# Stick-breaking sums in the rounded four-byte format, from a high and a low part of the softplus

## The reference, cut to what matters

```
z = jnp.einsum('bhqd,bhkd->bhqk', qb, kb) * scale
strict = k_pos < q_pos
log_keep = jnp.where(strict, jax.nn.log_sigmoid(-z), 0.0)
prefix = jnp.cumsum(log_keep, axis=-1)
after = prefix[..., -1:] - prefix
w = jnp.where(strict, jnp.exp(jax.nn.log_sigmoid(z) + after), 0.0)
outs.append(jnp.einsum('bhqk,bhkd->bhqd', w, vb))
```

## Time and profile before

| what | value |
|---|---|
| median of 3 runs | 1195.76 us (1193.81 to 1197.41) |
| the profiled run's own time | 1202.31 us |
| its span, first to last instruction | 1200.7 us |
| mean granted TensorE clock | 0.999 of full |
| TensorE matmuls, busy | 1185.0 us, 99% of the span |
| VectorE, ScalarE, GpSimd busy | 863.5, 636.0 and 95.4 us |

### The profile page before, as it was taken

The page is one execution under the profiler, slowest core; times in us unless marked ns, Lnnn a source line. Parts: engine busy times, 40 slices in busy tenths (PEclk is TensorE's granted clock), DMA queues, the critical chain, the costliest instruction groups (busy, mean ns, idle before and its releaser), DMA issues.

```text
span 1200.7 us, 23381 instructions
## 1 busy us (share of the span) xinstructions
PE 1185.0 (99%) x9643; PEld 1148.8 (96%) x9643; DVE 863.5 (72%) x1143; ACT 636.0 (53%) x853; POOL 95.4 (8%) x147
## 2 busy tenths in 40 slices
PE   8999999999999999999999999999999999999998
PEld 8999999999998999999999999999988779999998
DVE  5776887778776897777899888886476557755443
ACT  7557566634447567634468464333455665543432
POOL 0000010110124011110200001110000000000000
PEclk9999999999999999999999999999999999999999
DMA  9442587887772588787844648876745406565361
GB/s 335 159 175 72 178 290 269 297 291 253 263 263 72 176 270 291 277 289 275 294 171 141 203 149 281 286 254 204 235 142 193 157 1 187 166 210 178 124 193 66
DMA packets 150009, 249.98 MB, mean 208 GB/s; under 512 B 5505, under 2 KB 80618, under 8 KB 149930
## 3 DMA queue, kind: packets, MB, share of 16 engines
q1 hardware_dynamic: 135810, 198.21, 49.1%
q0 software_dynamic: 13952, 50.60, 11.7%
q10 hardware_dynamic: 168, 0.04, 0.0%
HBM read 247.79 MB, written 1.05 MB: 207 GB/s over the span
## 4 chain that ended last, share of the span: by engine, by line
PE 88%; DVE 8%; ACT 2%; issue 1%; ACTq 0%; POOL 0%; DVEq 0%
PE ps L2137 26%; PE ps L2139 26%; PE ps L2138 26%; DVE w_lo L1252 4%; PE ps L2405 2%; PE ps L2275 1%; PE ps L2693 1%; DVE scratch L1729 1%; PE ps L2387 1%; PE ps L2191 1%; ACT h_both L804 1%; PE ps L2667 1%; PE ps L2374 1%; PE ps L2707 1%; PE ps L2218 0%
## 5 line engine op out<-in xcount | busy, mean ns | idle before, releaser
L1252 DVE TENSOR_TENSOR w_lo<-raw,w_hi 128x2048 fp32r<-128x2048 f32 (+4 forms) x196 | 412.6, 2144 | 103.0 <-ACT w_hi L737 102.8
L737 ACT ACTIVATE w_hi<-raw 128x2048 fp32r<-128x2048 f32 (+4 forms) x196 | 342.0, 1790 | 169.0 <-PE ps L2139 168.9
L2137 PE MATMUL ps<-h_both,w_hi 128*128 128x256 f32 (+1 forms) x1296 | 363.8, 281 | 2.9 <-issue 1.1
L2139 PE MATMUL ps<-h_both,w_lo 128*128 128x256 f32 (+1 forms) x1296 | 361.3, 279 | 0.0
L2138 PE MATMUL ps<-h_both,w_hi 128*128 128x256 f32 (+1 forms) x1296 | 361.3, 279 | 0.0
L2137 PEld LDWEIGHTS ps<-h_both,w_hi 128*128 128x128 f32 (+1 forms) x1296 | 242.7, 187 | 4.3 <-issue 3.8
L2138 PEld LDWEIGHTS ps<-h_both,w_hi 128*128 128x128 f32 (+1 forms) x1296 | 244.2, 188 | 0.1
L2139 PEld LDWEIGHTS ps<-h_both,w_lo 128*128 128x128 f32 (+1 forms) x1296 | 244.1, 188 | 0.0
L2137 PE MATMUL ps<-a_both,w_hi 128*128 128x256 f32 x864 | 242.1, 280 | 0.0
L2139 PE MATMUL ps<-a_both,w_lo 128*128 128x256 f32 x864 | 241.4, 279 | 0.0
L2138 PE MATMUL ps<-a_both,w_hi 128*128 128x256 f32 x864 | 241.3, 279 | 0.0
(11 more groups left out here) (420 smaller groups left out, 1823.6 us busy)
## 6 DMA issues: line engine op xcount, KB each, us to landing
ada_raw<-in_l_ada_w POOLq DMA_DIRECT2D x96, 512.0 KB, 6.7
raw<-in_mlp_w_up SPq DMA_DIRECT2D x32, 1024.0 KB, 6.9
raw<-in_mlp_w_down SPq DMA_DIRECT2D x32, 1024.0 KB, 6.8
raw<-in_l_ffn_w_gate SPq DMA_DIRECT2D x22, 1024.0 KB, 5.4
raw<-in_l_ffn_w_up SPq DMA_DIRECT2D x22, 1024.0 KB, 8.0
raw<-in_l_ffn_w_down SPq DMA_DIRECT2D x16, 768.0 KB, 6.0
raw<-in_l_w_qkv SPq DMA_DIRECT2D x12, 1024.0 KB, 7.0
raw<-in_l_w_in SPq DMA_DIRECT2D x10, 1024.0 KB, 6.5
```

The costliest lines, as they stand in the source:

```text
L737: nc.scalar.activation(w_hi[:, s.slot, cut], raw[:, s.slot, cut], ACT.Copy).then_inc(split_hi, 1)
L1252: nc.vector.tensor_tensor(w_lo[:, s.slot, cut], raw[:, s.slot, cut], w_hi[:, s.slot, cut].bitcast(F32), ALU.subtract).then_inc(split_lo, 1)
L2137: nc.tensor.matmul(to, sh, mh, start=first, stop=False, skip_group_check=True)
L2139: return nc.tensor.matmul(to, sl, mh, start=False, stop=last, skip_group_check=True)
```

## The change

The softplus is split in a high part, rounded to `F32R`, and a low part, the rest. The sums become products of these two parts with constants in `F32R`: four products for each head, where there were two in the plain format.

- GpSimd copies each head's softplus into `sp_hi` (rounded) once `sp_ready` tells that it is there, and increments `sp_high`. From the third head on it first waits for the sums of the head two before.
- VectorE has a new step `softplus_low`: `sp_lo` = `sb_sp` - `sp_hi`, increments `sp_low`. Its order in iteration p is now `softplus(p + 1)`, `capped(p + 2)`, `softplus_low(p + 1)`, then `mix_low` as before.
- TensorE waits for `sp_low` in place of `sp_ready`, and uses `denied` in place of `suffix`.
- `sb_l` is gone: its steps work in `sb_w`, which has 8 places for heads in place of 4. `sb_sp`, `sp_hi` and `sp_lo` have 2 each. The waits on places are changed to match.
- `minus_ones` is made by a `tensor_scalar` in `F32R`, from `ones`, in place of a memset.

```
-            nc.gpsimd.memset(minus_ones[:, :], -1.0).then_inc(pool_step, 1)
+            nc.gpsimd.tensor_scalar(minus_ones[:, :], ones[:, :], -1.0, None, ALU.mult).then_inc(pool_step, 1)
...
+            for h in range(SB_HEADS):
+                pool.wait_ge(sp_ready, h + 1)
+                if h >= 2:
+                    pool.wait_ge(sums_ready, h - 1)
+                nc.gpsimd.tensor_copy(sp_hi[:, h % 2, :], sb_sp[:, h % 2, :]).then_inc(sp_high, 1)
...
-                    if h >= 4:
-                        dve.wait_ge(sp_ready, h - 3)
-                    nc.vector.tensor_scalar(sb_l[:, h % 4, :], ps[:, STICK_BANKS[h % 6], 0:384], FULL, None, ALU.min).then_inc(z_capped, 1)
+                    if h >= 8:
+                        dve.wait_ge(heads_done, len(HEADS) + h - 7)
+                    nc.vector.tensor_scalar(sb_w[:, h % 8, :], ps[:, STICK_BANKS[h % 6], 0:384], FULL, None, ALU.min).then_inc(z_capped, 1)
...
-                    if h >= 4:
-                        dve.wait_ge(sums_ready, h - 3)
-
-                    nc.vector.tensor_tensor(sb_sp[:, h % 4, :], ps[:, STICK_BANKS[h % 6], 0:384], sb_l[:, h % 4, :], ALU.max)                        .then_inc(sp_ready, 1)
+                    if h >= 2:
+                        dve.wait_ge(sp_low, h - 1)
+
+                    nc.vector.tensor_tensor(sb_sp[:, h % 2, :], ps[:, STICK_BANKS[h % 6], 0:384], sb_w[:, h % 8, :], ALU.max)                        .then_inc(sp_ready, 1)
+
+            def softplus_low(pair):
+
+                for h in (2 * pair, 2 * pair + 1):
+                    dve.wait_ge(sp_high, h + 1)
+                    nc.vector.tensor_tensor(sp_lo[:, h % 2, :], sb_sp[:, h % 2, :], sp_hi[:, h % 2, :].bitcast(F32), ALU.subtract)\
+                        .then_inc(sp_low, 1)
 
             capped(0)
             capped(1)
             softplus(0)
+            softplus_low(0)
             for p in range(SB_PAIRS):
                 if p + 1 < SB_PAIRS:
                     softplus(p + 1)
                 if p + 2 < SB_PAIRS:
                     capped(p + 2)
+                if p + 1 < SB_PAIRS:
+                    softplus_low(p + 1)
...
-                pe.wait_ge(sp_ready, h + 1)
-                z, sp_of = ps[:, STICK_BANKS[h % 6], :], sb_sp[:, h % 4, :]
-                nc.tensor.matmul(z[:, 0:384], suffix[:, :], sp_of, start=False, stop=False, skip_group_check=True)
-                nc.tensor.matmul(z[:, P:T], minus_ones[:, :], sp_of[:, T:T + P], start=False, stop=True,
-                                 skip_group_check=True).then_inc(sums_ready, 1)
+                pe.wait_ge(sp_low, h + 1)
+                z = ps[:, STICK_BANKS[h % 6], :]
+                for sp_of in (sp_hi[:, h % 2, :], sp_lo[:, h % 2, :]):
+                    nc.tensor.matmul(z[:, 0:384], denied[:, :], sp_of, start=False, stop=False, skip_group_check=True)
+                    ins = nc.tensor.matmul(z[:, P:T], minus_ones[:, :], sp_of[:, T:T + P], start=False, stop=False, skip_group_check=True)
+                ins.then_inc(sums_ready, 1)
```

More of the change, by code:

```diff
@@ L309, in build @@
         sb_kT = at("sb_kT", 8192, [P, KD, T])
[L310 to L316, removed]
+        sb_w = at("sb_w", 10240, [P, 8, 384])
+        sb_sp = at("sb_sp", 13312, [P, 2, 384])
+        sp_hi = at("sp_hi", 14080, [P, 2, 384], F32R)
+        sp_lo = at("sp_lo", 14848, [P, 2, 384], F32R)
+        suffix = at("suffix", 15616, [P, P])
+        minus_ones = at("minus_ones", 15744, [P, P], F32R)
+        denied = at("denied", 15872, [P, P], F32R)
+        far = at("far", 16000, [P, P], F32R)
         sb_sq = at("sb_sq", 12800, [P, NT, BANK])
@@ L370, in build @@
             sem("qk_sq"), sem("qk_var"), sem("qk_y"), sem("qk_scaled"), sem("qk_turned"), sem("qk_out"))
-        z_ready, z_capped, z_exped, z_soft, sp_ready, sums_ready, w_exped = (
-            sem("z_ready"), sem("z_capped"), sem("z_exped"), sem("z_soft"), sem("sp_ready"), sem("sums_ready"), sem("w_exped"))
+        z_ready, z_capped, z_exped, z_soft, sp_ready, sp_high, sp_low, sums_ready, w_exped = (
+            sem("z_ready"), sem("z_capped"), sem("z_exped"), sem("z_soft"), sem("sp_ready"), sem("sp_high"), sem("sp_low"),
+            sem("sums_ready"), sem("w_exped"))
         q_out, k_out, qk_banks = sem("q_out"), sem("k_out"), sem("qk_banks")
@@ L1198, in soft @@
                     act.wait_ge(z_capped, h + 1)
-                    nc.scalar.activation(sb_l[:, h % 4, :], sb_l[:, h % 4, :], ACT.Exp).then_inc(z_exped, 1)
+                    nc.scalar.activation(sb_w[:, h % 8, :], sb_w[:, h % 8, :], ACT.Exp).then_inc(z_exped, 1)
                 for h in (2 * pair, 2 * pair + 1):
                     act.wait_ge(z_exped, h + 1)
-                    nc.scalar.activation(sb_l[:, h % 4, :], sb_l[:, h % 4, :], ACT.Ln, bias=1.0).then_inc(z_soft, 1)
+                    nc.scalar.activation(sb_w[:, h % 8, :], sb_w[:, h % 8, :], ACT.Ln, bias=1.0).then_inc(z_soft, 1)
             def weights(pair):
@@ L1207, in weights @@
                     act.wait_ge(sums_ready, h + 1)
-                    if h >= 4:
-                        act.wait_ge(heads_done, len(HEADS) + h - 3)
-                    nc.scalar.activation(sb_w[:, h % 4, :], ps[:, STICK_BANKS[h % 6], 0:384], ACT.Exp).then_inc(w_exped, 1)
+                    nc.scalar.activation(sb_w[:, h % 8, :], ps[:, STICK_BANKS[h % 6], 0:384], ACT.Exp).then_inc(w_exped, 1)
             for j in range(6):
@@ L2707, in sb_values @@
                         ins = nc.tensor.matmul(ps[rows_of, 6 + g % 2, to], sb_rows[:, 2, kt, h * HD:(h + 1) * HD],
-                                               sb_w[:, h % 4, cut], start=pair % 2 == 0 and kt == 0, stop=pair % 2 == 1 and kt == 1,
+                                               sb_w[:, h % 8, cut], start=pair % 2 == 0 and kt == 0, stop=pair % 2 == 1 and kt == 1,
                                                skip_group_check=True)
```

## The result

The changed kernel took 1201.33 us in the median of 20 runs (1198.11 to 1206.97), the kernel before 1196.38 on the same chip: a ratio of 1.0041, 95% interval 1.0026 to 1.0056. It is slower by 0.4%, 4.95 us. The forecast was 1198.0 within 1193.5 to 1201.5, so the median is 3.3 us above it, 0.17 under the upper end of the range. Two further timings of the same pair on other chips gave ratios of 1.0002 (0.9983 to 1.0021) and 1.0035 (1.0012 to 1.0058).

What follows compares the result with a forecast made beforehand. TensorE was taken to bound the kernel, busy 99% of the span. First iteration +1.0, iterations 1 to 5 +1.0 and end +0.2 made +2.2: 1204.5 profiled, less 6.55 for the median, 1198.0 us, range 1193.5 to 1201.5.

Steps and rivals of the forecast that it cites:

- The loop: Attention iterations: sums, scores to `capped`, two `capped`, then subtraction and semaphore form one chain of 4.20 us, against 4.02.
- the two `capped`: VectorE, in the iteration's chain: two `capped` before the next instruction take 0.99 us.
- First iteration: Iteration 0 of the attention: 4.01 us against 3.02, adding 1.0 us.
- The products: TensorE sums: a head costs 0.57 us instead of 0.87, with 0.11 for each 128-column rounded product.
- Rival 2: TensorE sums: a rounded 128-column product costs 0.22 us, making the loop 4.64 and the time 1201.1; chance 0.17.
- the bound of 0.06: TensorE sums: lower bound in us for a rounded 128-column product, a third of the 384 columns' 0.17.
- The copies: GpSimd: 16 copies of 128 x 384 at 0.64 us each, hidden except at the end.
- rival 3: GpSimd copies are slow, 1.17 us each, adding 3.5 us in all, to 1199.3; chance 0.08.
- The end: Attention from 976.48 on: 6.3 us against 6.12, with the last subtraction waiting beside GpSimd's second copy.
- Rival 1: Attention: TensorE stays the limit and cheaper products save 4.8 us, giving 1191.0; chance 0.09.
- Rival 4, the clock: TensorE's clock falls to 1.2 GHz in new gaps, some 2.6 us in each of six iterations; chance 0.02.
- the forecast's own mark of 0.3%: Whole kernel: faster or slower means a difference of over 0.3%, 3.6 us; anything less counts as same.

Runs made afterwards that it cites:

- scores_first: Changed kernel with TensorE's order made scores, sums, values from iteration 1 and VectorE's made capped, softplus, low part; ratio to the kernel before 0.9967.
- copy_twice: Changed kernel with each GpSimd copy made twice, the second waiting on the first; attention 33.76 us against 30.30, no timed ratio given.
- before_scores_first: Kernel before (plain products) with the orders of scores_first, at one look; attention 28.37 and 28.36 us in this kernel's two runs.
- scores_first_pe: Changed kernel with only TensorE's order altered (scores, sums, values from iteration 1), VectorE's order kept; ratio to the kernel before 0.9995, attention 24.95 us.
- after_third: Changed kernel, unchanged, timed again on the same chip as filled_again; ratio to the kernel before 1.0035.
- filled: Changed kernel with TensorE's gaps filled by unused 128-column products, 12 in iteration 0, then 5; output no longer the reference's; ratio to the kernel before 1.0032.
- filled_again: The kernel filled, unchanged, timed again on the same chip as after_third; ratio to the kernel before 1.0022.
- low_first: Changed kernel with only VectorE's order altered, the low part directly behind softplus and ahead of capped; ratio to the kernel before 1.0032.
- after_again: Changed kernel, unchanged, run again on another chip; ratio to the kernel before 1.0002, attention 30.28 us.
- scores_first_pe_again: The kernel scores_first_pe, unchanged, timed again on another chip; ratio to the kernel before 0.9981.
- plain_scores_first: Kernel before (plain products) with the TensorE and VectorE orders of scores_first, now timed; ratio to the kernel before 0.9991.

## Why the forecast was nearly right, step by step

- **The loop.** Right, and its order shown by `scores_first`. I had 4.20; it is 1.30 + 1.27 + 0.94 + 0.60 = 4.11, over five iterations 0.45 us less. The one term that is off by more than 0.03 is the two `capped`: my row for it was two `softplus` with a `capped` behind them, 0.99, and two `capped` with a subtraction behind them take 0.94. First iteration: 4.01, as worked out. Idle TensorE: 0.66 in each, where I had 0.8.
- **The products.** Two neighbouring pairs of a 384-column and a 128-column product start 0.29 apart (at full clock 960.91 and 961.20), so a head costs 0.58 where I had 0.57, and a 128-column product some 0.12 where I had 0.11. The row of line 2405 was the right neighbour. Rival 2 (0.22) and the bound of 0.06 are out.
- **The copies.** Hidden, as said, and cheaper: see the row below, 0.51 against 0.64 (rival 3 is out). `copy_twice` shows the cover: with GpSimd at 1.98 us an iteration in place of 0.97 only iteration 6 and the end are longer.
- **The end.** 5.73 us where I had 6.3, the largest miss in size of any single term. The copies are shorter, and the wait of the subtraction beside the copy is 0.29, not 0.6.
- **Rival 1**, TensorE as the limit, came true only when the order was changed. I had 4.8 us saved in the products; TensorE's busy time falls by 4.7, from 28.37 in `before_scores_first` to 23.66 in `scores_first_pe`, and 1.3 of it is spent on the three waits that are left.
- **Rival 4, the clock: wrong in chance and in price.** I gave it 0.02 and 2.6 us in each of six iterations, "the gaps are short". By the count of mean clocks it falls in some 4 of 10 executions, and the fall in iteration 1, seen in `after_third` and in `copy_twice`, costs 1.54 us each time, once and not in six iterations. In the timed runs the executions of the changed kernel with a low mean clock are 1.0 us longer in the mean than the others of their group (groups as in the last section). Both stand behind the first gap, the longest (1.46), and that gap could have been read off the forecast: an iteration 0 of 4.01 with 2.6 of work in it.

For the measured difference, this gives +1.2 from the loop in every execution, and 18 / 44 x 1.54 = +0.6 from the clock in the mean, if those executions have one such fall each: +1.8. The forecast was +2.2 from the loop alone, 1.0 too much there and 0.6 too little by the clock that it left out. That the two sums are so near each other is luck. The two profiled executions, neither with a fall and both with the stretch of 164.93 us, bear out the first term: 1203.41 against 1202.31, 1.1 apart.

The timed difference is another matter. The three timings gave medians 4.95, 1.0 and 3.3 above the kernel before, and by the recorded ratios (1.0041, 1.0002, 1.0035) and the forecast's own mark of 0.3% the first and the third are slower, to which I gave 0.25, and only the second is the same, to which I gave 0.66. Much of what separates the three is the mix of two groups of times, some 6 us apart, that the last section describes: on the first chip 18 of 20 executions of the kernel before lie in the shorter group and 11 of 20 of the changed one. Group by group the changed kernel is 1.5 to 3.1 us longer, 2.7 in the middle of six comparisons, and 3.0 in the one with most executions on both sides. The forecast is one for the shorter group, since the 6.55 us that it takes off are about the distance of the two; in that group the changed kernel has 1199.36, 1.4 above the forecast.

So some 0.9 us is open between 1.8 and 2.7. `filled`, which has no falls, is 2.0 us longer in the middle of its three comparisons, with 1.2 in its attention, so 0.8 is open there too, and the clock is hardly its cause. No profile showed another stage that is longer by more than such stages scatter: the attention begins anywhere from 951.10 to 954.91 in the profiles. Whether the change has a part in which group an execution falls in isn't shown either: the longer group has 2 of 20 before and 9 of 20 after on the first chip, 30 of 35 and 6 of 12 on the second, 18 of 35 and 10 of 12 on the third.

GpSimd's copies and VectorE's subtractions in the changed kernel, ns shortest/median/longest:

```profile
L633 POOL CAST sp_hi<-sb_sp x16: 507/507/509, 948.6 to 979.0; 128x384 fp32r<-128x384 f32 x16
```

```profile
L2121 DVE TENSOR_TENSOR sp_lo<-sb_sp,sp_hi x16: 545/549/839, 949.1 to 979.9; 128x384 fp32r<-128x384 f32 x16
```

The 839 is the subtraction at 979.11, beside the copy that starts at 979.03. The Trainium skill, "SBUF — State Buffer", section "Who interferes with whom", has the one of such a pair that was issued first keep the other out for its whole duration. The direction agrees: the copy came first and the subtraction was longer. By it alone, I estimate, the subtraction would have waited to the end of the copy at 979.54, 0.43; it lost 0.29.

## What to carry to other kernels

Before making a busy engine's work cheaper, follow what it waits for through the other engines' orders. Here a new step stood behind one that waits for the same iteration's scores, and turned 4.02 - 3.45 = 0.57 us of work saved per iteration into 0.66 us idle; moving one call on TensorE gave it back. Gaps that open in a fully busy TensorE stretch can have a second price. Here both falls in iteration 1 that were profiled stood behind the longest gap, so list the gaps one by one and not only their mean, and look at the clock of many executions: of three profiles of the changed kernel one shows it. And before two medians are compared, look at whether the times come in groups.

## What the runs showed of the hardware

**Two spacings of the same products.** Far behind the attention, in code that is the same in all these kernels, the stretch from a 0.71 us pause near 1030 to the last gated addition takes 164.93 us in some executions and 158.76 in others. Both occur with one kernel; these are pieces of the chain that ended last in `filled` and in `filled_again`:

```profile
1031.35 0.71 issue
...
1190.11 0.50 DVE xT L2030
```

```profile
1031.63 0.71 issue
...
1196.56 0.49 DVE xT L2030
```

It is 164.93 too in the first profiles of the kernel before and of the changed one. The granted clock reads 1.00 in either. TensorE's products of 256 columns start 0.114 apart in the one and 0.118 in the other, and both spacings can stand within one execution (`low_first`: 0.114 near 989, 0.118 near 1100). I have not tried what decides it. It moves a run by 6 us, more than this change does, and its share differs from chip to chip: the kernel before had medians of 1196.38, 1201.86, 1196.79 and 1200.64 on four.

Sorted, the times of each kernel on one chip fall in two groups, or lie all in one, and the profiled executions of the nine rows below each lie in the group of their stretch: from the end of the attention to the last gated addition it is 205.2 us in the two in shorter groups, 211.3 to 211.7 in the seven in longer ones. Medians of each group in us, with the number of executions:

| kernel | shorter: before, this | longer: before, this |
|---|---|---|
| changed, first timing | 1196.33 (18), 1199.36 (11) | 1204.01 (2), 1205.50 (9) |
| `after_again` | 1196.89 (5), 1199.47 (6) | 1202.72 (30), 1205.86 (6) |
| `after_third` | 1196.09 (17), 1198.83 (2) | 1202.17 (18), 1204.28 (10) |
| `filled` | 1196.79 (23), 1198.75 (9) | none, 1204.78 (3) |
| `filled_again` | 1196.09 (17), 1198.51 (2) | 1202.17 (18), 1204.01 (10) |
| `scores_first` | 1196.89 (5), 1194.83 (6) | 1202.72 (30), 1201.08 (6) |
| `scores_first_pe` | 1196.79 (23), 1194.54 (10) | none, 1201.36 (2) |
| `scores_first_pe_again` | 1196.09 (17), 1193.04 (3) | 1202.17 (18), 1198.65 (9) |
| `plain_scores_first` | 1196.09 (17), 1195.46 (6) | 1202.17 (18), 1201.11 (6) |

Read this way, `scores_first` (2.1 and 1.6 less) and `plain_scores_first` (0.6 and 1.1 less) come near to what their profiles show in the attention, 2.2 and 0.75.
